# Head variances' inverse roots on GpSimd, and convolved tiles cast one or two loop steps sooner, in a two-block fp32 transformer kernel

## What is computed

```python
def second_block(x, ...):
    h = rmsnorm_2(x, norm_mix_pre)
    dq, dk, dvv, mq, mk, mv, mo, mi, mf = split(h @ w_in)
    o_diff = diff_attention(rope(dq), rope(dk), dvv, lam)
    o_diff = rmsnorm_2(o_diff, diff_norm) * (1.0 - lam_init)   # x * rsqrt(mean(x * x) + EPS), per head and token
    qk = silu(causal_dwconv(concat(mq, mk), conv_w, conv_b))
    mq, mk = qk[..., :256], qk[..., 256:]
    hm = mlstm_chunkwise(mq, mk, mv, mi + b_igate, log_sigmoid(mf + b_fgate))
    o_mlstm = rmsnorm_2(hm, mlstm_norm) * sigmoid(mo)
    x = x + rmsnorm_2(concat(o_diff, o_mlstm) @ w_out, norm_mix_post)
    h = rmsnorm_2(x, norm_mlp_pre)
    return x + rmsnorm_2(square(relu(h @ w_up)) @ w_down, norm_mlp_post)
```

## Time and profile before

| | |
|---|---|
| median of 3 runs | 1536.5 us (1536.28 to 1536.57) |
| profiled execution, its own time | 1536.2 us |
| its span in the trace | 1534.4 us |
| TensorE (PE) busy | 1512.8 us, 99% |
| VectorE (DVE) busy | 739.3 us, 48% |
| ScalarE (ACT) busy | 564.2 us, 37% |
| GpSimd (POOL) busy | 80.1 us, 5% |
| granted TensorE clock, mean | 0.999 |

### The profile page before, as it was taken

One profiled execution on the slowest core, in us unless ns is written; L12 is line 12 of the kernel. 1 busy time (PEld: TensorE's weight loads), 2 busy tenths in 40 slices (PEclk: granted clock), 3 DMA queues, 4 the chain that ended last, 5 costly groups with the idle time before them and its releaser, 6 DMA issues.

```text
span 1534.4 us, 18870 instructions
## 1 busy us (share of the span) xinstructions
PE 1512.8 (99%) x7006; PEld 1228.8 (80%) x7006; DVE 739.3 (48%) x1068; ACT 564.2 (37%) x917; POOL 80.1 (5%) x70
## 2 busy tenths in 40 slices
PE   9999999999999999999999999999999999999998
PEld 7888888887885688888888887866788888888886
DVE  5444433347346664444323466576657542244434
ACT  5322211224325543222212265346745443134322
POOL 0000000002005120000000033200000000000000
PEclk9999999999999999999999999999999999999999
DMA  6333353334221133333333343520223332333222
GB/s 190 98 99 97 98 138 96 96 96 122 83 82 47 56 110 96 96 96 96 96 96 96 96 110 104 184 71 28 83 87 120 110 96 96 97 96 96 96 97 96
DMA packets 247833, 151.19 MB, mean 99 GB/s; under 512 B 18128, under 2 KB 230752, under 8 KB 247520
## 3 DMA queue, kind: packets, MB, share of 16 engines
q1 hardware_dynamic: 234432, 143.67, 31.8%
q10 hardware_dynamic: 13344, 6.75, 1.6%
HBM read 144.10 MB, written 5.78 MB: 98 GB/s over the span
## 4 chain that ended last, share of the span: by engine, by line
PE 92%; DVE 3%; ACT 2%; issue 1%; DMA 1%; SPq 0%; DVEq 0%; ACTq 0%
PE bank L366 29%; PE bank L370 29%; PE bank L369 29%; DVE w_low L1149 1%; PE bank L2070 1%; PE bank L2122 1%; DMA region_f<-in_x 1%; PE bank L2081 1%; PE bank L2290 0%; ACT w_high L631 0%; PE bank L2009 0%; PE bank L2236 0%; PE bank L2154 0%; PE bank L2133 0%; PE bank L1866 0%
## 5 line engine op out<-in xcount | busy, mean ns | idle before, releaser
L366 PE MATMUL bank<-region,w_high 128*128 128x512 f32 (+2 forms) x1492 | 585.7, 393 | 5.0 <-DVE w_low L1149 1.4
L370 PE MATMUL bank<-region,w_low 128*128 128x512 f32 (+2 forms) x1492 | 579.4, 388 | 0.0
L369 PE MATMUL bank<-region,w_high 128*128 128x512 f32 (+2 forms) x1492 | 579.0, 388 | 0.0
L1149 DVE TENSOR_TENSOR w_low<-w_raw,w_high 128x1024 fp32r<-128x1024 f32 (+1 forms) x259 | 334.4, 1297 | 154.0 <-ACT w_high L631 150.2
L631 ACT CAST w_high<-w_raw 128x1024 fp32r<-128x1024 f32 (+1 forms) x259 | 265.7, 1027 | 265.2 <-DMA w_raw<-in_ffn_w_down 107.4
L366 PEld LDWEIGHTS bank<-region,w_high 128*128 128x128 f32 (+1 forms) x1492 | 279.7, 187 | 67.9 <-issue 4.6
L370 PEld LDWEIGHTS bank<-region,w_low 128*128 128x128 f32 (+1 forms) x1492 | 279.5, 187 | 59.0
L369 PEld LDWEIGHTS bank<-region,w_high 128*128 128x128 f32 (+1 forms) x1492 | 279.8, 188 | 55.8
L366 PE MATMUL bank<-w_high,region 128*128 128x512 f32 x416 | 164.5, 395 | 2.8 <-DVE w_low L1149 1.5
L370 PE MATMUL bank<-w_high,region 128*128 128x512 f32 x416 | 162.2, 390 | 0.0
L369 PE MATMUL bank<-w_low,region 128*128 128x512 f32 x416 | 162.0, 389 | 0.0
(11 more groups left out here) (252 smaller groups left out, 1063.4 us busy)
## 6 DMA issues: line engine op xcount, KB each, us to landing
w_raw<-in_ffn_w_down SPq DMA_DIRECT2D x48, 512.0 KB, 3.8
w_raw<-in_ffn_w_gate SPq DMA_DIRECT2D x44, 512.0 KB, 3.8
w_raw<-in_ffn_w_up SPq DMA_DIRECT2D x44, 512.0 KB, 3.8
w_raw<-in_w_in SPq DMA_DIRECT2D x40, 512.0 KB, 3.9
w_raw<-in_w_up SPq DMA_DIRECT2D x32, 512.0 KB, 4.0
w_raw<-in_w_down SPq DMA_DIRECT2D x32, 512.0 KB, 3.3
w_raw<-in_w_out SPq DMA_DIRECT2D x16, 512.0 KB, 3.7
region_f<-in_x SPq DMA_DIRECT2D x4, 512.0 KB, 7.3
```

What stands on the lines that cost most here:

```text
L366: mm = pe.matmul(out, a_hi, b_hi, start=start, stop=False)
L369: pe.matmul(out, a_hi, b_lo, start=False, stop=False)
L370: return pe.matmul(out, a_lo, b_hi, start=False, stop=stop)
L1149: last = dve.tensor_tensor(piece(w_low[b % RING]), piece(w_raw[b % RING]), piece(w_high[b % RING]).bitcast(F32), ALU.subtract)
```

## The change

The inverse root of the 16 head variances is no longer a root on ScalarE and a reciprocal on VectorE: GpSimd raises them to the power of a tile `neg_half` that holds -0.5 and that it has filled itself. It signals `e_rec` in VectorE's place. `conv_hi` moves from the loop steps 13, 15, 17, 18 to 13, 14, 16, 17 on ScalarE, and `conv_lo` from 15, 16, 18, 19 to 15, 16, 17, 18 on VectorE.

```diff
+        neg_half = sb("neg_half", [P, TT * DH])
...
+        power_in = sem("exponents_in")
...
-                if w in (13, 15, 17, 18):
-                    conv_hi(CONV_ORDER[(13, 15, 17, 18).index(w)])
+                if w in (13, 14, 16, 17):
+                    conv_hi(CONV_ORDER[(13, 14, 16, 17).index(w)])
...
-                if u == 1:
-                    act.wait_ge(e_var, 1)
-                    act.activation(head_std[:, 0:TT * DH], head_std[:, 0:TT * DH], ACT.Sqrt).then_inc(e_std, 1)
...
-                if w in (15, 16, 18, 19):
-                    conv_lo(CONV_ORDER[(15, 16, 18, 19).index(w)])
+                if w in (15, 16, 17, 18):
+                    conv_lo(CONV_ORDER[w - 15])
...
-                if u == 2:
-                    dve.wait_ge(e_std, 1)
-                    dve.reciprocal(head_rstd[:, 0:TT * DH], head_std[:, 0:TT * DH]).then_inc(e_rec, 1)
...
+            pool.memset(neg_half[:], -0.5).then_inc(power_in, 1)
+            pool.wait_ge(power_in, 1)
+            pool.wait_ge(e_var, 1)
+            pool.tensor_tensor(head_rstd[:, 0:TT * DH], head_std[:, 0:TT * DH], neg_half[:], ALU.pow).then_inc(e_rec, 1)
```

## The result

The changed kernel takes 1538.68 us in the median of its runs, the kernel before 1536.56 us in those beside it: a ratio of 1.0013, with a 95% interval of 1.0007 to 1.0019. The forecast was 1534.9 us, with a range up to 1538.0. So the change costs 2.1 us where it was to give 1.6 us, and the time lies outside the range. The difference is clear of noise, but under the 0.2% that the prediction took as its bound for "same". One of the 22 runs of the changed kernel took 3617.57 us and is left out of the ratio; the other 21 lie between 1538.20 and 1540.41 us.

What follows compares the result with a forecast made beforehand. TensorE was taken as the bound, busy 1512.8 of 1534.4 us. Root -1.47, power 0 and casts -0.08 made -1.55 us, from 1536.5 to 1534.9 us; range 1534.2 to 1538.0, to hold 8 in 10.

Steps and rivals of the forecast that it cites:

- same: Outcome within 0.2%, 3.07 us, of the kernel before; chance 0.85, against faster 0.02 and slower 0.13.
- moves forward as a block: Behind u = 3 in the second loop, TensorE's waits follow its own order, so all the rest keeps the gain.
- The root: ScalarE's root and table loads go, so TensorE's spreading of the maxima at u = 3 starts 1.47 us sooner (1.31 to 1.57).
- the detour of 2.82 us: ScalarE's table load, root and load back, 1091.07 to 1093.89; 1.35 us of it was never on the path.
- The power: GpSimd's power behind the variances takes 2 us, hidden, cost 0; range 0.2 to 8 us, or 0 to +3.1 us.
- The slack of 4.9 us: GpSimd's time from the variances until TensorE loads the inverse roots; only what the power takes beyond it counts, one for one.
- Rival A: The power is dear, 10 to 40 us lane by lane, and TensorE stands at u = 4; over 9.5 us: chance 0.12.
- Rival B: GpSimd's first power loads code, some 6 us, giving 1538.0 or 1536.3 us; with a power of 5 to 9.5 us: 0.11.
- The casts: First loop: wait for `value_raw` at w = 15 grows 1.30 us, won back at the squares, w = 20; sum -0.08 us.
- Rival C: `value_raw` is late by 1.30 us and the wait at w = 20 stays as long: 1536.3 us; chance 0.05.
- The clock: Sign in the profile after: granted clock 0.999 as before.

Runs made afterwards that it cites:

- e2_before_64: The kernel before with only an unused tile of 64 bytes where the change puts `neg_half`: 1540.30 us, ratio 1.0026.
- e4_rest_64: The kernel before with an unused tile of 64 bytes right ahead of `f3_rest`, so that this tile alone moves: 1540.79 us, ratio 1.0029.
- g1_power_only: The changed kernel with the casts at their old places and `f3_rest` 256 bytes above its old place: 1535.59 us, ratio 0.9993 to the kernel before.
- e6_conv_only: The kernel before with the new places of `conv_hi` and `conv_lo` alone, root still on ScalarE, no new tile: 1537.34 us, ratio 1.0002.
- g3_keep_keys: The changed kernel with `f3_rest` 256 bytes above its old place and `conv_hi` at w = 13, 15, 16, 17: 1533.32 us, ratio 0.9979 to the kernel before.
- f2_ring_64: The kernel before with the weight tiles moved by 64 bytes against the regions and `f3_rest` by 256: 1567.69 us, ratio 1.0206.
- h1_regions_64: The kernel before with x and the regions 64 bytes off both weights and `f3_rest` modulo 256: 1555.47 us in one run, against 1537.55 us beside it.
- g2_three_powers: The changed kernel with casts at old places, `f3_rest` 256 bytes up and the power done three times in sequence: 1542.37 us, ratio 1.0035 to the kernel before.

## Why the prediction was wrong

- **The missing step.** It costed `neg_half` in one clause, that its filling is hidden. It is: 0.10 us while GpSimd has nothing to do. But a tile has a place as well as a price in instructions, and each tile that is allocated behind it moved by 64 bytes. That was no term of the sum, and it costs 4.4 us in the trace (e2_before_64: 4.0 us, e4_rest_64: 4.5 us in the medians). The sentence that TensorE's rest "moves forward as a block" is where it failed: it did so up to 1188 us, and not in the stages that read `f3_rest`: 226.7 ns a matmul became 232.8 ns. Nothing in a profile of the kernel before shows that such a price exists; that the addresses move stood in the diff.
- **The range and the rivals.** Its upper end was made of the power's price alone, and none of the rivals was this. That "same" came true was luck: a gain of about 2 us and a loss of 4.4 us, for a reason that the prediction didn't name.
- **The root.** Forecast 1.47 us (1.31 to 1.57), measured 1.47 us at the spreading of the maxima itself in the changed kernel (from 0.49 to 1.96 us ahead) and 1.48 us in g1_power_only. With the matmul behind it, 1.57 and 1.58 us: the upper end was the better figure, since the next start moves by 0.10 us more. Both loads of tables are gone (one that starts at 1127.37 is another, at 1129.42 before), and of the detour of 2.82 us the rest wasn't on the path, as said.
- **The power.** Estimated 1 to 3 us with 2 us taken, measured 2.94 us, then 2.90 us. The slack of 4.9 us held: no wait with one power, and with three the matmul came 3.65 us late where 3.9 us were expected. Rival A was real, only far off (its 10 to 40 us stood on no row): it decides at 4.9 us, and a power of this shape takes 2.9 us. Rival B fell: the first power of an execution takes 2.93 us and the next two 2.90 us. The Trainium skill, "GPSIMD Engine Reference", section "Instruction dispatch", gives some 6 us for a first call to freshly loaded code; the trace has nothing like it here.
- **The casts.** Forecast -0.08 us, measured -0.28 us at the squares in the changed kernel, -0.29 us in e6_conv_only, and -0.36 us behind them in both. The mechanism was right in both halves: 1.81 us of waiting for `value_raw`, and none for the squares. Rival C fell. The size was off by 0.3 us: TensorE came to the squares at 1083.20 and not at 1083.54. The changed execution was ahead by 0.14 us already; and the prediction carried the whole 1.30 us of w = 15 on to w = 20, while 0.18 us of it was won back on the way, 0.16 us at the sums of the head before (1075.85 in the trace of before). In the runs the part gains nothing that can be told: e6_conv_only's median is 1.0 us above the kernel before. g3_keep_keys shows what it was worth without its first half: its matmuls are 1.35 us further ahead at the squares than before them.
- **The clock.** I had named the granted clock only as a thing that would stay. It does in the mean, 0.999, but these short waits can be followed by a stretch at 1.2 GHz; I did not expect it to follow waits of 1.3 and 1.8 us in some executions.

## What to carry to other kernels

Count a new tile as a move of all that is laid out behind it: compare the start addresses of the operands that TensorE reads at full pace, and where a sum of waits doesn't close, compare the starts of the same instructions in both traces, since a slower pace shows in no wait and in no share of busy time. Here full pace was seen only where the activation tiles and the weight tiles agreed modulo 256 bytes. And when work is moved to another loop step, look at each wait that it is moved past: here two of the three moves (the last two casts, as in g3_keep_keys) were worth some 1.3 us, and the third gave most of it back.

## What the runs showed of the hardware

- Matmuls of fp32 with 512 columns, issued back to back at the granted clock of 1.00, were 226.7 ns apart when the tiles of both operands left the same at a division of their addresses by 256, 228.9 ns when the streamed tile started 64 bytes above the loaded one, and 233.3 ns when it started 64 bytes below (f2_ring_64, h1_regions_64). Where two activation tiles that disagreed took turns, it was 231.1 to 232.8 ns, by the distance. With the weights moved by 64 bytes against the regions (f2_ring_64) this made 31 us. Why it is so stays open: the runs show the distances 0, 32, 64, 128, 192 and 256 bytes and no mechanism inside.
- A power on GpSimd over 128 x 16 elements took 2.90 to 2.94 us (3.0 us from start to start in g2_three_powers, the wait between them included), over ten times the 0.22 us of a simple product of that shape.
- Behind waits of 1.3 to 3.5 us of TensorE the granted clock was 0.50 for about 3.4 us, and 6.8 us behind the longest, in some executions. In g1_power_only 3.4 us at that clock cost 0.66 us, as TensorE's wait of 0.8 us for `w_low` was gone with it; in g2_three_powers the 6.8 us cost 2.5 us.
